# Block-product feed-forward on one core: order of the weight loads, the first two down loads on another condition, two low parts ahead of the sums in tile 4

## The reference, cut to what matters

```
def swiglu(h, w_gu, w_down):
    gu = h @ w_gu
    g, u = gu[..., :D_FF], gu[..., D_FF:]
    return (jax.nn.silu(g) * u) @ w_down
...
for l in range(DEPTH):
    x = x + 0.5 * swiglu(rmsnorm(x, ffn1_norm[l]), ffn1_w_gu[l], ffn1_w_down[l])
    x = x + hybrid_mixing(...)
    x = x + 0.5 * swiglu(rmsnorm(x, ffn2_norm[l]), ffn2_w_gu[l], ffn2_w_down[l])
```

## Time and profile before

| | us |
|---|---|
| runs shown | 2761.19 median (2758.33 to 2762.11), 3 runs |
| the profiled execution: device time | 2760.55 |
| its span, first to last instruction | 2758.3 |
| PE busy | 2715.7 (98% of the span) |
| DVE busy | 1995.7 (72%) |
| ACT busy | 1254.6 (45%) |
| mean share of the 16 DMA engines, queue of SP | 24.6% |
| mean granted TensorE clock | 0.997 |

### The profile page before, as it was taken

How to read it: one execution, slowest core, us unless ns; L and a number is a source line. 1 busy time by engine, 2 the same in 40 slices (tenths; PEclk the granted TensorE clock), 3 DMA queues, 4 the chain that set the end, 5 groups by cost and what they waited for, 6 DMA issues and landing times.

```text
span 2758.3 us, 47695 instructions
## 1 busy us (share of the span) xinstructions
PE 2715.7 (98%) x18638; PEld 2311.5 (84%) x18638; DVE 1995.7 (72%) x3036; ACT 1254.6 (45%) x1975; POOL 237.3 (9%) x191
## 2 busy tenths in 40 slices
PE   9999999999999999999999999999999999999998
PEld 7999876778998889998767899987878665789997
DVE  7888756577887678875656788867766776678875
ACT  4444535454444544444445444455344112445444
POOL 0000012010000100001301000001101431100002
PEclk9999999999999999999999999999999999999999
DMA  3323231122322223223112233232201221222322
GB/s 142 112 98 101 87 104 43 39 96 96 107 102 92 90 105 104 96 99 107 55 36 95 92 102 108 88 119 69 77 26 35 78 91 59 84 96 95 106 93 92
DMA packets 57006, 242.37 MB, mean 88 GB/s; under 512 B 6473, under 2 KB 10889, under 8 KB 38049
## 3 DMA queue, kind: packets, MB, share of 16 engines
q1 hardware_dynamic: 54896, 233.51, 24.6%
q10 hardware_dynamic: 1568, 6.64, 0.7%
q0 software_dynamic: 400, 0.23, 0.0%
HBM read 238.34 MB, written 2.10 MB: 87 GB/s over the span
## 4 chain that ended last, share of the span: by engine, by line
PE 88%; DVE 6%; DMA 3%; ACT 2%; issue 1%; POOL 0%; SPq 0%; POOLq 0%; DVEq 0%; ACTq 0%; PEldq 0%
PE psum L655 86%; DVE ring_lo L2372 2%; DMA ring<-in_wgu 2%; PE psum L1195 1%; DMA ring<-in_wd 1%; DVE hid L2776 1%; ACT highs L1761 0%; ACT highs L1839 0%; POOL scr L3399 0%; DVE scr L2735 0%; DVE h_lo L2394 0%; DVE scr L2739 0%; DVE highs L2372 0%; ACT L1847 0%; PE psum L1430 0%
## 5 line engine op out<-in xcount | busy, mean ns | idle before, releaser
L655 PE MATMUL psum<-highs 128*128 128x512 f32 (+2 forms) x3560 | 1135.3, 349 | 18.2 <-DVE highs L2372 11.1
L655 PEld LDWEIGHTS psum<-highs 128*128 128x128 f32 x3560 | 666.2, 190 | 116.8 <-issue 25.9
L655 PE MATMUL psum<-h_lo,highs 128*128 128x256 f32 (+1 forms) x2200 | 701.9, 319 | 0.0
L655 PE MATMUL psum<-highs,ring_lo 128*128 128x512 f32 (+1 forms) x1272 | 474.9, 388 | 0.0
L655 PEld LDWEIGHTS psum<-h_lo,highs 128*128 128x128 f32 x2200 | 418.1, 190 | 31.2 <-issue 0.5
L2372 DVE TENSOR_TENSOR ring_lo<-ring,highs 128x1024 fp32r<-128x1024 f32 (+3 forms) x173 | 267.1, 1545 | 98.8 <-ACT highs L1761 60.5
L655 PEld LDWEIGHTS psum<-highs,ring_lo 128*128 128x128 f32 x1272 | 238.1, 187 | 50.5 <-issue 0.5
L1885 ACT ACTIVATE highs<-ring 128x1024 fp32r<-128x1024 f32 x90 | 95.4, 1060 | 298.7 <-PE psum L655 298.7
L655 PE MATMUL psum<-highs,scr_r 128*128 128x256 f32 x720 | 203.7, 283 | 0.0
L655 PE MATMUL psum<-highs,hid_r 128*128 128x256 f32 x720 | 203.7, 283 | 0.0
L655 PE MATMUL psum<-highs,wdr_lo 128*128 128x512 f32 x488 | 190.8, 391 | 0.0
(11 more groups left out here) (463 smaller groups left out, 5273.7 us busy)
## 6 DMA issues: line engine op xcount, KB each, us to landing
ring<-in_wgu SPq DMA_DIRECT2D x105, 1024.0 KB, 5.1
wdr<-in_wd SPq DMA_DIRECT2D x110, 256.0 KB, 2.6
ring<-in_wd SPq DMA_DIRECT2D x25, 1024.0 KB, 4.8
ring<-in_wmix SPq DMA_DIRECT2D x28, 512.0 KB, 3.5
ring<-in_wmix SPq DMA_DIRECT2D x12, 1024.0 KB, 5.0
ring<-in_wproj SPq DMA_DIRECT2D x22, 512.0 KB, 3.5
ring<-in_wmix SPq DMA_DIRECT2D x8, 768.0 KB, 4.4
ring<-in_wgu SPq DMA_DIRECT2D x10, 512.0 KB, 5.9
```

The lines of the kernel that those rows point to most:

```text
L655: return nc.tensor.matmul(o, w, r, start=start, stop=stop, skip_group_check=True)
```

## The change

Three edits of order, and one wait that goes with the second. Nothing is added to or taken from the arithmetic.

1. SP: from tile 5 on, the ring load of a tile is issued ahead of the `wdr` load of the tile before it. The loop is rotated: it issues `blocked_item(j)` and then `wd_item(j-1)`.
2. SP: down items 0 and 1 are issued when the content of their slots (tiles 20 and 21) has been split, not when PE has finished these tiles. `wd_item(21)` stands between them. ACT now waits for the end of tile 21 (`ring_free`) before it writes the high part of item 1, which the load's own wait saw to before.
3. DVE: in tile 4 (`first`), `low_hid(3)` and `low_t4` come ahead of `sum1(5)`. In the other tiles the order stays.

```
-                for j in range(2, PLAIN + 2):
+                for j in range(2, PLAIN):
                     gu_item(f, j, (j + par) % 2, n0 + j)
                     wd_item(f, j, j % 2, f * NJ + j)
+                gu_item(f, PLAIN, par, n0 + PLAIN)
+                gu_item(f, PLAIN + 1, 1 - par, n0 + PLAIN + 1)
+                wd_item(f, PLAIN, 0, f * NJ + PLAIN)
                 with sp.Fori(PLAIN // 2 + 1, NJ // 2) as jj:
                     for s in range(2):
                         blocked_item(f, n0, 2 * jj + s, (s + par) % 2)
-                        wd_item(f, 2 * jj + s, s, f * NJ + 2 * jj + s)
-                for i in range(6):
+                        wd_item(f, 2 * jj + s - 1, 1 - s, f * NJ + 2 * jj + s - 1)
+                sp.wait_ge(ring_split, blocks_split(n0, NJ - 2, 3))
+                sp.dma_start(ring[:, par, 0:DOWN_COLS[0]], wd2[f, 0][:, 0:DOWN_COLS[0]]).then_inc(ring_in[par], 16)
+                wd_item(f, NJ - 1, 1, f * NJ + NJ - 1)
+                sp.wait_ge(ring_split, blocks_split(n0, NJ - 1, 3))
+                sp.dma_start(ring[:, 1 - par, 0:DOWN_COLS[1]], wd2[f, 1][:, 0:DOWN_COLS[1]]).then_inc(ring_in[1 - par], 16)
+                for i in range(2, 6):
                     sp.wait_ge(ring_free, n0 + NJ + i + 1)
...
                         it = NEXT_ITEM[k]
+                        if it == 1:
+                            act.wait_ge(ring_free, used(n0 + NJ - 1))
                         split_ring(n0 + NJ + it, gu_hi[:, (it + par) % 2, :], DOWN_COLS[it])
...
-                    if not last:
+                    if first:
+                        low_hid(j - 1, 1 - s)
+                        low_t(t4_lo, blocks(t4), t4_hi, 4)
+                        weight_sums(j + 1, 1 - s)
+                    elif not last:
                         sum1(j + 1, 1 - s)
-                    low_hid(j - 1, 1 - s)
-                    if first:
-                        low_t(t4_lo, blocks(t4), t4_hi, 4)
-                    if not last:
+                        low_hid(j - 1, 1 - s)
                         later_sums(j + 1, 1 - s)
+                    else:
+                        low_hid(j - 1, 1 - s)
```

## The result

| | before | changed |
|---|---|---|
| median | 2759.73 (2758.33 to 2762.11), 6 runs | 2740.28 (2739.86 to 2740.95), 6 runs |
| the profiled execution: device time | 2760.55 | 2740.87 |
| its span | 2758.3 | 2739.0 |

A forecast was written before the change was run, and what follows sets the result against it. The prediction took PE to bound the kernel nearly throughout, stalling in tile 4 and at k = 2. Savings of 14.5 + 5.4 = 19.9 us took the span from 2758.3 to 2738.4, forecasting a 2740.7 median, range 2736.5 to 2747.

The forecast's parts named there:

- term of 5.4 us for k = 2: Start of the down loop: issuing item 1 earlier ends PE's waits at k = 2, 5.4 us over five parts.
- 14.5 for tile 4: Tile 4: the early load of tile 5 and DVE's order together bring back 14.5 us over five parts.
- So all three waits in tile 4 end.: Tile 4: PE no longer waits for `low_hid(3)`, for u3 ahead of `fourth`, or for tile 5's low tops.
- The forecast for e2, about 8: Tile 4, made for e2: DVE's order alone brings back 8 of the 14.5 us, 2751.5.
- PE, which never waited there, gains 0: Tiles 5 to 21: DVE's ring load waits, about 1 us a tile, end, and PE gains 0.
- Down items: Start of the down loop: item 0 gains 0; item 1 goes out at 291.3, leaving PE 1.3 us to spare.
- new wait for item 2: Down loop, at k = 6: a PE wait for item 2 would have shown the prediction wrong.
- The likeliest case: Whole kernel: all of the forecast gain comes back, from 2737 to 2744 us, chance 0.75.
- a drop of the clock elsewhere: Behind a remaining short wait: TensorE's clock drops, about 1.7 us a drop, giving 2742 to 2744; chance 0.07.
- 1.7 of part 1's 3.78 us: Tile 4 of part 1: the half clock behind the stall cost 1.7 of the 3.78 us lost there.

The follow-up runs named there:

- e3: Kernel before with only down items 0 and 1 issued when their slots are split, with ACT's wait: 2753.99 us, ratio 0.9977.
- e1: Kernel before with only tile 5's ring load moved ahead of tile 4's `wdr` load: 2747.32 us, ratio 0.9952.
- e9: The changed kernel measured once more, unaltered, on one chip with e10 and e11: 2739.04 us, ratio 0.9923 to the kernel before.
- e4: Kernel before with tile 5's ring load held back until tile 4's `wdr` load has landed: 2769.83 us, ratio 1.0032.
- e2: Kernel before with only DVE's order in tile 4 changed, loads as before: 2752.07 us, ratio 0.9968.
- e5: Changed kernel with DVE's order in tile 4 put back to that of before: 2737.83 us, ratio 0.9921.
- e10: Repeat of e5, the changed kernel without DVE's new order, on one chip with e9 and e11: 2739.36 us, ratio 0.9923.
- e8: Kernel before with only the loop order from tile 6 on changed, ring load ahead of the previous tile's `wdr` load: 2759.1 us, ratio 0.9999.
- e11: Repeat of e6, the two SP edits alone, on one chip with e9 and e10: 2742.18 us, ratio 0.9933.
- e6: Kernel before with tile 5's ring load early and only down item 1 issued on its split, with ACT's wait: 2739.56 us, ratio 0.9926.
- e7: Kernel before with DVE's tile 4 order and both early down items, ring and `wdr` loads as before: 2745.55 us, ratio 0.9947.

## Why the prediction was right

- **The time.** Forecast 2740.7, measured 2740.28. For the term of 5.4 us for k = 2, e3 alone gave 6.7; for the term of 14.5 for tile 4, e1 gave 13.4 by its median and 14.5 by its trace. The medians together make 20.1, against 19.9 forecast and 19.5 and 21.4 measured (e9).
- **What held tile 4.** Shown from both sides: the load earlier by one place takes the stall away (e1), the load held back, so that it lands later, lengthens the waits by 8.4 us in all (e4). The prediction followed the wait of PE to DVE, from DVE to the load, and from the load to SP's place behind another load's wait.
- **"So all three waits in tile 4 end."** They did. Where margins were given they held: the forecast gave `low_tops(5)` 1.2 us ahead of PE; it ended at 77.96 + 1.75 = 79.71, and PE's first product began 0.24 ahead of 81.00, at 80.76: 1.05 to spare. `low_hid(3)` ended at 71.55, some 3.6 us before PE had come to `down1(3)`. The load went out 0.8 us later than worked out, as all of part 1 did (40.53 against 39.69), and took 4.7 us, not the 5.83 that the prediction carried over; the margins did not need this.
- **Its third edit bought nothing.** The prediction took the edits of tile 4 as one, and so gave the 14.5 to the load and the order together. Apart they are not equal: the load alone brings it (e1), the order alone 8.6 (e2), and the order on top of the load nothing that can be measured (e5 and e10 against the changed kernel; tile 4 takes 5.98 us in both traces). The forecast for e2, about 8, came from the u3 rows and was right.
- **Tiles 5 to 21, where "PE, which never waited there, gains 0".** Right to within what the medians show: e8 gave 0.9999 with an interval of 0.001, 2.5 us, to either side, although 63.6 us of DVE's waits ended. It was not exact. The prediction read the unbroken chain of part 1; in part 5 of the same trace one steady tile took 6.20 us behind a ring load of 7.25, and the traces put the loop's worth at 0.2 to 1.7 us an execution (under e8).
- **Down items.** `low_down(2)` ended at 304.90 + 0.68 = 305.58 and k = 2 began at 306.94: 1.4 us to spare, forecast 1.3. Item 1 went out at 288.43: the 291.3 worked out, less the 2.9 us by which the part was ahead there (3.78 gained, 0.84 lost at the start). No new wait for item 2 came.
- **The clock.** The likeliest case had no drop that was not there before. The profiled execution had one, behind `kn_tok`, at 1.6 us: the rival "a drop of the clock elsewhere", whose price was put at 1.7. It hardly shows in the total because stretches 1 to 3 and 5 gave 0.16, 0.59, 0.60 and 0.24 us more than forecast, 1.6 in all, against 1.4 lost in the fourth and 0.84 at the start: that the total is right within half a microsecond is partly luck. Most of that surplus is in rows. In the second stretch PE's wait of 0.63 us for POOL's `scr` at 947.92 shrank to 0.15; in the third its wait of 0.33 us for `scr_r` at 988.91 went, 0.5 with the restart; in the fifth the steady tile that had lost 0.22 lost nothing. The other tenths I have not traced.
- **The share of the clock in tile 4.** The prediction put 1.7 of part 1's 3.78 us down to the half clock. That is what the slow matmuls took longer, not what the drop cost. Beyond PE's wait for `low_hid` itself, part 1 lost 3.78 - 1.95 = 1.83 us and the other four parts, without a drop, 1.55 or 1.56 each: the drop cost 0.3. The wait of 0.6 us ahead of `fourth` is missing in part 1 alone, which fits: the slow matmuls filled time in which PE would otherwise have stood. The 14.5 is not touched by this, since it was measured as a whole.

## What to carry to other kernels

Follow a stall through every queue: PE waited for DVE, DVE for a load, and the load for its place behind another load's wait, and the edit at that last link (one line of SP's order) gave all that the edit at the middle link gave and more. An operation moved ahead of a waiting one rescues only itself; ask which of those behind it are wanted next. And a wait is worth what the engine that is late loses by it: 63.6 us of DVE's waits went for under 1 us, 11.1 us of PE's, with what hung on them, for 19.5. Such waits cost nothing here as long as the loads took their usual 5 us, and some tenths of a microsecond or more where one took 7 or more.

## What the runs showed of the hardware

Whether TensorE falls to its lower clock behind a short stall was not set by the stall's length. In e4 the five stalls of tile 4 were between 2.92 and 3.12 us, in the same code; the windows (columns as above) show the drop in parts 1, 3 and 4, and parts 2 and 5 have none:

```profile
75.00:100.00 25.00, 21.88 (x148) 20.47 (x148) 21.30 (x32) 10.99 (x15) 0.00 (x0) 0.93 0.32 117
1000.00:1025.00 25.00, 22.04 (x149) 20.43 (x148) 20.49 (x31) 10.07 (x14) 0.00 (x0) 0.93 0.31 117
1575.00:1600.00 25.00, 23.34 (x159) 21.98 (x160) 22.62 (x34) 11.40 (x16) 0.00 (x0) 0.93 0.29 106
```

The wait of 2.23 us for `kn_tok` was followed by a drop in the changed kernel, e1, e4, e5, e8, e9 and e11, and by none in the kernel before, e2, e3, e6, e7 and e10 (seven profiled executions of thirteen). In each of the seven, PE came to the next group of `kn_tok` matmuls 1.6 us later than without a drop (27.3 or 27.4 us behind the first group instead of 25.7), whichever matmuls ran slowly. In tile 4 a drop cost less: beyond PE's wait itself, the three parts of e4 with a drop lost 1.80 to 1.82 us and the two without 1.55 and 1.56. That fits a price that depends on whether PE would have stood behind the drop anyway. The seven of thirteen fit what the Trainium skill says (TensorE: Matmul & The Clock Gate, Part 1: The HAM clock gate), that the monitor runs freely, so that the moment counts; no run here moves a stall in time and nothing else, so it is not shown. Its practical side is: an edit anywhere ahead can move a drop of 1.6 us in or out, and differences of that size between versions (e9 to e11) should not be read as the edit's.
